# A weight ring of twenty 1 MB slots in place of ten 2 MB slots, in a two-layer diffusion backbone with a mixture of experts

## The chip, the cores and the metric

The kernel runs on one core of one Trainium2 chip. The metric is the device time of one execution in microseconds, lower is better. Everything is float32.

## What is computed

Two layers act on 256 latent tokens of 1024 values. Layer 0 mixes tokens by differential attention over latent and context tokens, layer 1 by centred pooling. After each mixer comes a mixture of 16 experts of which every token uses two. Cut to the part that the change touches:

```python
def moe_ffn(h, router_w, router_b, wg, wu, wd):       # h: 256 x 1024; wg, wu, wd: 16 x 1024 x 1024
    eidx, ew = route(h, router_w, router_b)           # two experts and two weights for each token
    ...                                               # the tokens of one expert are gathered into xb
    def expert_block(args):
        xb, e = args
        return (jax.nn.silu(xb @ wg[e]) * (xb @ wu[e])) @ wd[e]
    ...                                               # weighted sum back into the tokens

for i in range(DEPTH):                                # DEPTH = 2
    yl = diff_attention(...) if i % 4 == 0 else pool_mixer(hl, pool_w[j], pool_scale[j])
    xl = deepnorm_update(xl, yl, g1, ln_g[i, 0], ln_b[i, 0])
    y2 = moe_ffn(xl * (1.0 + sc2) + sh2, router_w, router_b, moe_wg[i], moe_wu[i], moe_wd[i])
    xl = deepnorm_update(xl, y2, g2, ln_g[i, 1], ln_b[i, 1])
```

The kernel computes every expert for its own tokens, in up to 64 slots for each expert. The weights of the experts are 2 layers x 16 experts x 3 matrices x 4 MiB = 402.65 MB, all of which must be read once from memory.

## The kernel before

The program is written by hand for each engine, with semaphores between them. The order of work on an engine is the order of the code.

**The ring.** `ring` is one SBUF buffer of RING = 10 slots, each of UNIT = 4096 values on each of 128 partitions, which is 2 MB (2.097 million bytes). A **unit** is one half of one expert matrix: 512 rows of 1024 values. An expert has EU = 6 units: two of moe_wg, two of moe_wu, two of moe_wd. Units are numbered through the program by v: 0 to 95 are layer 0's experts, 96 (POOL_UNIT) is the pooling layer's tables, 97 to 192 are layer 1's experts. `ring_slot` (L270) gives unit v the slot (v + 2) mod 10 and the number of times that this slot has been filled.

**Loading.** SP issues all weight DMAs, in order of v (`load_expert`, L391). In front of each stands `slot_free` (L376): the first ten units wait for parts of the attention that use the ring as scratch, and all others wait until unit v - 10 has been used (`used`, L279). One DMA brings a whole unit. Partition p gets the rows 4p to 4p + 3 of the half matrix, which lie next to one another in memory, so one partition's share is one run of 16 KB. Each DMA ends with an increment of `ring_loaded_{slot}`.

**Using.** On PE, `expert` (L785) runs for each expert: gate (bank 4) and up (bank 5) products from four units, then a gather of later tokens (L735), turning the hidden values (L759) and the slot weights (L765), the down product (bank 6) from two units, and the scatter (L751). A unit is used by `two_halves` (L739): four k-steps, each a pair of matmuls that write different halves of the partitions, so eight matmul instructions; the profile records each of them twice, so a unit is 16 of its MATMUL records (L743). `ring_unit` (L776) waits for the landing of the unit (`landed`), and the last matmul increments `unit_used`. ACT (L1050) takes the sigmoid once the gate product is complete (`used(act, v + 1)`), DVE (L1481) multiplies once the up product is complete (`used(dve, v + 3)`), copies the turned hidden values (L1496), and scales the down product (L1500, `used(dve, v + 5)`).

**Between the layers.** After expert 15 of layer 0 comes `pool_layer` (L845). Unit 96 holds pool_w (1 MB, as 1024 rows of 1 KB) in the first half of its slot, and the band table (128 rows of 4352 bytes) in the second; two DMAs with two semaphores, `pool_loaded` and `ring_loaded_{slot}`. POOL multiplies pool_w by a gate (L445) once it has landed. Before the pooling PE runs four matmuls whose result is not used (`keep_clock`, L682). `further_loads` and `further_experts` are loops for experts with more than 64 tokens; with these inputs they don't run.

The packing of rows to partitions in `load_expert`:

```python
src = (moe_wg, moe_wu, moe_wd)[n // 2][layer, e, (n % 2) * HALF:(n % 2 + 1) * HALF, :]
load(slot(s).rearrange("p (k n) -> p k n", k=4), src.rearrange("(p k) n -> p k n", p=P), sem(f"ring_loaded_{s}"))
```

Of the kernel before, what the change touches and what calls it, by code (L numbers as in the profile page):

```python
# [26 lines left out]
P = 128  # L27
D = 1024
KT = D // P
TOK = 256  # L30
TT = TOK // P
NB = 512
HALF = D // 2
# [16 lines left out]
UNIT = 4096  # L50
EU = 6
BAND = P + 8

# [11 lines left out]

POOL_UNIT = NE * EU
LAYER_BASE = [0, POOL_UNIT + 1]
PAIRS = NE // 2
# [77 lines left out]
def trunk(nc, x, c, ctx, c_ctx, mod_w, mod_b, ln_g, ln_b, attn_wqkv, attn_wo, attn_lam, attn_subln,  # L146
          pool_w, pool_scale, router_w, router_b, moe_wg, moe_wu, moe_wd, consts, rope, band, out):
    with ExitStack() as st:
# [121 lines left out]
        def ring_slot(v):  # L270

            return (v + SHIFT) % RING, v // RING + 1

# [46 lines left out]
        def first_unit(layer, e):  # L320

            return LAYER_BASE[layer] + e * EU

# [30 lines left out]
        def _(sp):  # L354
# [20 lines left out]

            def slot_free(v):  # L376

                if v < 2:
                    sp.wait_ge(sem("summed"), NSUM - 1 + v)
                elif v < 6:  # L380
                    sp.wait_ge(sem("oT_done"), 2 * TT)
                elif v == 6:
                    sp.wait_ge(sem("mix_done"), 2)
                elif v == 7:
                    normed(sp, 0, 1)
                elif v < RING:
                    sp.wait_ge(sem("unit_used"), NA - RING + v + 1)
                else:
                    used(sp, v - RING)

            def load_expert(layer, e):  # L391
                for n in range(EU):
                    v = first_unit(layer, e) + n
                    slot_free(v)
                    s, _ = ring_slot(v)
                    src = (moe_wg, moe_wu, moe_wd)[n // 2][layer, e, (n % 2) * HALF:(n % 2 + 1) * HALF, :]
                    load(slot(s).rearrange("p (k n) -> p k n", k=4), src.rearrange("(p k) n -> p k n", p=P),
                         sem(f"ring_loaded_{s}"))

# [11 lines left out]
            for layer in range(DEPTH):  # L411
                for e in range(NE):
                    load_expert(layer, e)
                further_loads(layer)
                if layer == 0:
                    slot_free(POOL_UNIT)
                    s, _ = ring_slot(POOL_UNIT)
                    load(slot(s)[:, 0:2048].rearrange("p (k n) -> p k n", k=KT),
                         pool_w[0].rearrange("g (k p) n -> p (g k) n", p=P), sem("pool_loaded"))
                    load(slot(s)[:, 2048:2048 + TT * 4 * BAND], band, sem(f"ring_loaded_{s}"))  # L420
            for t in range(TT):
# [8 lines left out]
        def _(pool):  # L430
# [9 lines left out]
            pool.wait_ge(sem("job_out"), 7)  # L440
            pool.wait_ge(sem("pool_loaded"), 16)
            pw = slot(ring_slot(POOL_UNIT)[0])[:, 0:2048].rearrange("p (g k n) -> p g k n", g=4, k=2)
            for g in range(4):
# [5 lines left out]
        def _(pe):  # L449
# [288 lines left out]

            def two_halves(b, lhs, w, k0):  # L739

                for k in range(4):
                    for h in range(2):
# [33 lines left out]
            def ring_unit(v):  # L776
                landed(pe, v)
                return slot(ring_slot(v)[0]).rearrange("p (k n) -> p k n", k=4)

# [5 lines left out]
            def expert(layer, e):  # L785
# [6 lines left out]
                for b in range(2):  # L792
                    for n in range(2):
                        if e2 == 0 and (b, n) == (0, 1):
                            pe.wait_ge(sem("xg_copied"), 4 * (gq + 2 * pr_ + 2))
                        two_halves(4 + b, x_in, ring_unit(v + 2 * b + n), 4 * n).then_inc(sem("unit_used"), 1)
                if pr_ + 1 < PAIRS:
# [12 lines left out]
                elif layer == DEPTH - 1:  # L810
                    pe.wait_ge(sem("lng_copied"), e2 + 1)
                for n in range(2):
                    two_halves(6, h_tile, ring_unit(v + 4 + n), 4 * n).then_inc(sem("unit_used"), 1)
                pe.wait_ge(sem("ys_ready"), q + 1)
# [30 lines left out]
            def pool_layer():  # L845

                v = POOL_UNIT
                pe.wait_ge(sem("pool_loaded"), 16)
                landed(pe, v)
                w = slot(ring_slot(v)[0])  # L850
                pw = w[:, 0:2048].rearrange("p (k n) -> p k n", k=KT)
                bd = w[:, 2048:2048 + TT * 4 * BAND].rearrange("p (t g n) -> p t g n", t=TT, g=4)
                keep_clock(5, 4)
# [16 lines left out]
                for t in range(TT):  # L870
                    for h in range(2):
# [10 lines left out]
                        if (t, h) == (1, 1):  # L882
                            last.then_inc(sem("unit_used"), 1)
                        pe.wait_ge(sem("xT8_act"), KT + 2 * h + 2)
# [22 lines left out]
        def _(act):  # L907
# [142 lines left out]
            def expert(layer, e):  # L1050
                v = first_unit(layer, e)
                used(act, v + 1)
                nc.scalar.activation(sig, bank(4), ACT.Sigmoid).then_inc(sem("sig_ready"), 1)  # L1053
# [53 lines left out]
        def _(dve):  # L1107
# [373 lines left out]
            def expert(layer, e):  # L1481
# [10 lines left out]
                dve.wait_ge(sem("silu_ready"), q + 1)  # L1492
                used(dve, v + 3)
                v_.tensor_tensor(hmid, hmid, bank(5), ALU.mult).then_inc(sem("h_ready"), 1)  # L1494
                dve.wait_ge(sem("hT_turned"), q + 1)
                v_.tensor_copy(work[:, NB:2 * NB], bank(7)).then_inc(sem("hTt_copied"), 1)  # L1496
                if e + 1 < NE:
                    weights_out(q + 1)
                used(dve, v + 5)
                v_.tensor_tensor(ysb, bank(6), gt[layer], ALU.mult).then_inc(sem("ys_ready"), 1)  # L1500
# [78 lines left out]
```

## Time and profile before

| | us |
|---|---|
| median of three runs | 1286.6 |
| lowest and highest run | 1284.5, 1288.28 |
| the profiled execution, its whole time | 1288.75 |
| the profiled execution, its span | 1286.4 |

PE is busy for 1178.4 us of the span, DVE for 379.5, ACT for 169.1 and POOL for 23.0. The granted clock of PE is full in most of the span.

The stages, by the timeline: conditioning and attention to 334 us; the first norm, the router and the first gathers to 355; experts of layer 0 from 355 to 792; norm, pooling, second norm and router to 837; experts of layer 1 from 837 to 1274; the last norm and the stores to 1286. To read the profile for this case, two clocks have to be laid side by side: at what pace PE uses the units, and at what pace the DMAs bring them. The first is read from the chain of waits, the second from the time of issue and the time to landing of single DMAs and from the windows, whose last number is the rate in GB/s.

### The profile page before, as it was taken

What the parts mean: (1) busy time and instruction counts of PE and PEld (TensorE: products, weight loads), DVE (VectorE), ACT (ScalarE), POOL (GpSimd) and SP (SyncE); (2) the same over time, 40 slices, a digit from 0 to 9 for tenths busy, and PEclk for the clock granted to TensorE, in tenths of its full rate; (3) what the DMA queues carried; (4) which work ended last, traced back from release to release, by engine and by line L of the source; (5) the groups of instructions that cost most, each with busy time, mean ns of one, the idle gap of its engine ahead of it and who ended that gap; (6) DMA issues with size and microseconds to landing.
All of it is one profiled execution on the core that took longest, in us unless ns stands there. A gap on an engine that the chain in (4) does not pass through costs nothing.

```text
span 1286.4 us, 12344 instructions
## 1 busy us (share of the span) xinstructions
PE 1178.4 (92%) x5277; PEld 508.7 (40%) x5277; DVE 379.5 (29%) x781; ACT 169.1 (13%) x398; POOL 23.0 (2%) x28
## 2 busy tenths in 40 slices
PE   5999999889899999999999998999999999999995
PEld 1444344445543343333343334733343333333331
DVE  1497898872411111111111103411111111111113
ACT  0201123341310010000010002410010000010000
POOL 0001100000000000000000001000000000000000
PEclk9799999968899999999999999899999999999998
DMA  9778868701999999999999999989999999999993
GB/s 326 290 260 297 325 234 294 287 2 51 430 383 429 427 428 428 427 428 427 427 428 427 429 427 418 419 366 428 426 429 427 430 425 429 426 428 429 425 428 165
DMA packets 54940, 476.27 MB, mean 370 GB/s; under 512 B 5034, under 2 KB 6458, under 8 KB 30308
## 3 DMA queue, kind: packets, MB, share of 16 engines
q1 hardware_dynamic: 42632, 433.04, 80.4%
q0 software_dynamic: 10560, 41.94, 8.9%
q8 instruction: 44, 0.72, 0.2%
q10 hardware_dynamic: 1692, 0.46, 0.2%
q14 instruction: 12, 0.10, 0.0%
HBM read 474.38 MB, written 1.05 MB: 370 GB/s over the span
## 4 chain that ended last, share of the span: by engine, by line
PE 76%; DMA 11%; DVE 9%; issue 2%; ACT 2%; SPq 0%; DVEq 0%
PE ps L743 47%; PE ps L535 5%; PE ps L735 5%; DMA ring<-in_mod_w 5%; PE ps L751 4%; DMA ring<-in_moe_wu 3%; DMA ring<-in_moe_wd 3%; DVE modp L1164 3%; PE ps L600 2%; PE ps L564 2%; DVE work L1496 2%; DVE work L1500 2%; PE ps L458 1%; PE ps L759 1%; PE ps L582 1%
## 5 line engine op out<-in xcount | busy, mean ns | idle before, releaser
L743 PE MATMUL ps<-ring,tra 128*64 128x512 f32 x2048 | 447.0, 594 | 3.0 <-DMA ring<-in_moe_wu 1.9
L743 PEld LDWEIGHTS ps<-ring,tra 128*64 128x64 f32 x2048 | 145.9, 137 | 299.1 <-issue 293.1
L743 PE MATMUL ps<-ring,work 128*64 128x512 f32 x1024 | 227.2, 595 | 29.4 <-DVE work L1496 29.2
L743 PEld LDWEIGHTS ps<-ring,work 128*64 128x64 f32 x1024 | 82.7, 137 | 153.2 <-issue 115.4
L535 PE MATMUL ps<-ring 128*128 128x512 f32 x320 | 141.6, 596 | 0.7 <-ACT ring L935 0.7
L1164 DVE SCALAR_TENSOR_TENSOR modp<-ring,modp 128x512 f32<-128x512 f32 x140 | 105.3, 752 | 5.0
L1491 DVE TENSOR_TENSOR work<-ps,work 128x512 f32<-128x512 f32 x32 | 22.1, 692 | 283.4 <-ACT work L1053 283.4
L535 PEld LDWEIGHTS ps<-ring 128*128 128x128 f32 x320 | 59.3, 190 | 77.4 <-issue 76.4
L1053 ACT ACTIVATE work<-ps 128x512 f32<-128x512 f32 x32 | 19.1, 597 | 532.7 <-PE ps L743 532.7
L751 PE MATMUL ps<-work,extra 64*128 64x512 f32 x256 | 63.6, 615 | 25.1 <-DVE work L1500 25.1
L1046 ACT ACTIVATE tra<-ps,cols 128x128 f32<-128x128 f32 x128 | 48.2, 456 | 246.4 <-PE ps L735 246.4
L1494 DVE TENSOR_TENSOR work<-work,ps 128x512 f32<-128x512 f32 x32 | 22.0, 688 | 182.0 <-PE ps L743 182.0
L735 PEld LDWEIGHTS ps<-extra,xn 128*128 128x128 f32 x512 | 65.0, 206 | 25.6 <-issue 22.7
L735 PE MATMUL ps<-extra,xn 128*128 128x128 f32 x512 | 70.7, 296 | 2.7 <-DVE extra L1405 2.7
L751 PEld LDWEIGHTS ps<-work,extra 64*128 64x128 f32 x256 | 22.0, 186 | 68.4 <-DVE work L1500 53.3
L1500 DVE TENSOR_TENSOR work<-ps,gt 128x512 f32<-128x512 f32 x16 | 11.1, 692 | 115.7 <-PE ps L743 115.7
L1500 DVE TENSOR_TENSOR work<-ps,rows 128x512 f32<-128x512 f32 x16 | 11.1, 692 | 115.4 <-PE ps L743 115.4
L1496 DVE COPY work<-ps 128x512 f32<-128x512 f32 x32 | 22.1, 692 | 51.0 <-PE ps L759 51.0
L989 ACT ACTIVATE work<-ps,small 128x512 f32<-128x512 f32 x32 | 21.7, 683 | 67.6 <-DVE small L1302 67.6
L508 PE MATMUL ps<-modp,cst 128*12 128x512 f32 x40 | 21.6, 623 | 5.5 <-DVE modp L1164 3.0
L1301 DVE TENSOR_REDUCE small<-ps 128x2 f32<-128x1024 f32 x16 | 19.5, 1221 | 11.9 <-PE ps L564 11.8
L564 PE MATMUL ps<-ring 64*128 64x512 f32 x64 | 22.7, 792 | 0.0
(177 smaller groups left out, 651.0 us busy)
## 6 DMA issues: line engine op xcount, KB each, us to landing
ring<-in_moe_wg SPq DMA_DIRECT2D x64, 2048.0 KB, 25.7
ring<-in_moe_wu SPq DMA_DIRECT2D x64, 2048.0 KB, 24.7
ring<-in_moe_wd SPq DMA_DIRECT2D x64, 2048.0 KB, 24.0
ring<-in_mod_w POOLq DMA_DIRECT2D x20, 2048.0 KB, 9.6
ring<-in_attn_wqkv SPq DMA_DIRECT2D x6, 2048.0 KB, 13.8
ring<-in_mod_w SPq DMA_DIRECT2D x4, 2048.0 KB, 18.6
ring<-in_attn_wo SPq DMA_DIRECT2D x2, 2048.0 KB, 9.1
xn<-in_x SPq DMA_DIRECT2D x1, 1024.0 KB, 17.2
```

What stands on the lines that cost most here:

```text
L535: last = mm(bank(g % 2), hT[:, k, t * P:t * P + P], w[:, k, :], start=(k == 0), stop=(k == KT - 1))
L564: last = mm(bank(score_bank(s) + n), qT[j][rows_n, h, t * P:t * P + P], kT[rows_n, HPJ * j + h, :], start=True, stop=True)
L600: last = mm(bank(2 * t + h), oT[t][:, k, :], wo[:, k, :], start=(k == 0), stop=(k == KT - 1))
L735: last = mm(bank(bk, 0, P, k * P, k * P + slots), xn[:, c0:c0 + P], sgat[:, t, 0:slots], start=(t == 0), stop=(t == TT - 1), skip_group_ch ...
L743: last = mm(ps[SLOTS * h:SLOTS * h + SLOTS, b, :], lhs(k0 + k), w[:, k, h * NB:(h + 1) * NB], start=(k0 + k == 0), stop=(k0 + k == KT - 1) ...
L751: last = mm(bank(2 * t + h), sw[SLOTS * h:SLOTS * h + SLOTS, t * P:t * P + P], ysb[SLOTS * h:SLOTS * h + SLOTS, :], start=False, stop=True ...
L1046: nc.scalar.activation(xg[i // 2 % 2][:, kk, :], bank(bk, k * P, k * P + P), ACT.Identity, bias=one(bcol[2 * layer], kk, 1), scale=one(aco ...
L1164: ins = v_.scalar_tensor_tensor(out=acc, in0=w[:, k, :], scalar=ck, in1=acc, op0=ALU.mult, op1=ALU.add)
L1491: v_.tensor_tensor(hmid, bank(4), sig, ALU.mult).then_inc(sem("silu_ready"), 1)
L1494: v_.tensor_tensor(hmid, hmid, bank(5), ALU.mult).then_inc(sem("h_ready"), 1)
L1496: v_.tensor_copy(work[:, NB:2 * NB], bank(7)).then_inc(sem("hTt_copied"), 1)
L1500: v_.tensor_tensor(ysb, bank(6), gt[layer], ALU.mult).then_inc(sem("ys_ready"), 1)
```

## The change

A slot is now handled as two halves of 1 MB. Units keep their places in the ring, but the numbers v now count halves ("parts"): an expert has PARTS = 12, the ring HALVES = 20, the pooling tables are parts 192 and 193, layer 1 begins at 194. Each part has its own DMA, its own `ring_loaded_{s}` semaphore, its own wait on PE and its own increment of `unit_used`. Part n of a unit brings the rows 4p + 2n and 4p + 2n + 1 to partition p, a run of 8 KB; the runs of one DMA now lie 16 KB apart in memory. The matmuls, their order and their operands stay as they are. The first twenty parts wait for what the first ten units waited for. The tables of the pooling layer get one part each, and band's DMA now waits for its own part's release; `pool_loaded` goes.

```diff
+HALVES = 2 * RING
+PARTS = 2 * EU
...
-            return (v + SHIFT) % RING, v // RING + 1
+            return (v + 2 * SHIFT) % HALVES, v // HALVES + 1
+
+        def half_slot(s):
+
+            return ring[:, s * UNIT // 2:(s + 1) * UNIT // 2]
...
-            def slot_free(v):
-
+            def slot_free(part):
+
+                v = part // 2
...
-                    used(sp, v - RING)
+                    used(sp, part - HALVES)
...
-                for n in range(EU):
+                for n in range(PARTS):
                     v = first_unit(layer, e) + n
                     slot_free(v)
                     s, _ = ring_slot(v)
-                    src = (moe_wg, moe_wu, moe_wd)[n // 2][layer, e, (n % 2) * HALF:(n % 2 + 1) * HALF, :]
-                    load(slot(s).rearrange("p (k n) -> p k n", k=4), src.rearrange("(p k) n -> p k n", p=P),
-                         sem(f"ring_loaded_{s}"))
+                    i, k0 = n // 2, n % 2 * 2
+                    src = (moe_wg, moe_wu, moe_wd)[i // 2][layer, e, (i % 2) * HALF:(i % 2 + 1) * HALF, :]
+                    load(half_slot(s).rearrange("p (k n) -> p k n", k=2),
+                         src.rearrange("(p k) n -> p k n", p=P)[:, k0:k0 + 2, :], sem(f"ring_loaded_{s}"))
...
-                    load(slot(s)[:, 0:2048].rearrange("p (k n) -> p k n", k=KT),
-                         pool_w[0].rearrange("g (k p) n -> p (g k) n", p=P), sem("pool_loaded"))
-                    load(slot(s)[:, 2048:2048 + TT * 4 * BAND], band, sem(f"ring_loaded_{s}"))
+                    load(half_slot(s).rearrange("p (k n) -> p k n", k=KT),
+                         pool_w[0].rearrange("g (k p) n -> p (g k) n", p=P), sem(f"ring_loaded_{s}"))
+                    slot_free(POOL_UNIT + 1)
+                    load(half_slot(s + 1)[:, 0:TT * 4 * BAND], band, sem(f"ring_loaded_{s + 1}"))
...
-            def two_halves(b, lhs, w, k0):
-
-                for k in range(4):
+            def two_halves(b, lhs, w, k0, count=4):
+
+                for k in range(count):
...
-                return slot(ring_slot(v)[0]).rearrange("p (k n) -> p k n", k=4)
+                return half_slot(ring_slot(v)[0]).rearrange("p (k n) -> p k n", k=2)
...
-                    for n in range(2):
-                        if e2 == 0 and (b, n) == (0, 1):
+                    for n in range(4):
+                        if e2 == 0 and (b, n) == (0, 2):
                             pe.wait_ge(sem("xg_copied"), 4 * (gq + 2 * pr_ + 2))
-                        two_halves(4 + b, x_in, ring_unit(v + 2 * b + n), 4 * n).then_inc(sem("unit_used"), 1)
+                        two_halves(4 + b, x_in, ring_unit(v + 4 * b + n), 2 * n, 2).then_inc(sem("unit_used"), 1)
...
-                for n in range(2):
-                    two_halves(6, h_tile, ring_unit(v + 4 + n), 4 * n).then_inc(sem("unit_used"), 1)
+                for n in range(4):
+                    two_halves(6, h_tile, ring_unit(v + 8 + n), 2 * n, 2).then_inc(sem("unit_used"), 1)
...
                         if (t, h) == (1, 1):
-                            last.then_inc(sem("unit_used"), 1)
+                            last.then_inc(sem("unit_used"), 2)
...
-                used(act, v + 1)
+                used(act, v + 3)
...
-                used(dve, v + 3)
+                used(dve, v + 7)
...
-                used(dve, v + 5)
+                used(dve, v + 11)
```

In SP's queue, at the start of layer 0's experts, this stood before (a row is a DMA, its shape, what it waits for, and how many alike follow):

```order
L356 DMA ring<-in_moe_wg 128x4096 [waits summed] x2
L356 DMA ring<-in_moe_wu 128x4096 [waits oT_done] x2
L356 DMA ring<-in_moe_wd 128x4096 [waits oT_done] x2
L356 DMA ring<-in_moe_wg 128x4096 [waits mix_done]
L356 DMA ring<-in_moe_wg 128x4096 [waits norm_dve,norm_act]
L356 DMA ring<-in_moe_wu 128x4096 [waits unit_used] x2
L356 DMA ring<-in_moe_wd 128x4096 [waits unit_used] x2
```

And this stands there now:

```order
L362 DMA ring<-in_moe_wg 128x2048 [waits summed] x4
L362 DMA ring<-in_moe_wu 128x2048 [waits oT_done] x4
L362 DMA ring<-in_moe_wd 128x2048 [waits oT_done] x4
L362 DMA ring<-in_moe_wg 128x2048 [waits mix_done] x2
L362 DMA ring<-in_moe_wg 128x2048 [waits norm_dve,norm_act] x2
L362 DMA ring<-in_moe_wu 128x2048 [waits unit_used] x4
L362 DMA ring<-in_moe_wd 128x2048 [waits unit_used] x4
```

The order of the matrices and the kinds of waits are the same; every DMA has become two of half the size. On PE, at the beginning of the first expert of layer 0, this stood before:

```order
L743 MATMUL ps<-ring,tra 64x512 [waits ring_loaded_2,swT_copied,xg_copied]
L743 MATMUL ps<-ring,tra 64x512 x7
L743 MATMUL ps<-ring,tra 64x512 [waits ring_loaded_3,xg_copied]
L743 MATMUL ps<-ring,tra 64x512 x7
L743 MATMUL ps<-ring,tra 64x512 [waits ring_loaded_4]
```

And this now:

```order
L752 MATMUL ps<-ring,tra 64x512 [waits ring_loaded_4,swT_copied,xg_copied]
L752 MATMUL ps<-ring,tra 64x512 x3
L752 MATMUL ps<-ring,tra 64x512 [waits ring_loaded_5]
L752 MATMUL ps<-ring,tra 64x512 x3
L752 MATMUL ps<-ring,tra 64x512 [waits ring_loaded_6,xg_copied]
L752 MATMUL ps<-ring,tra 64x512 x3
L752 MATMUL ps<-ring,tra 64x512 [waits ring_loaded_7]
```

The matmuls are the same ones in the same order; a wait for a landing stands after every fourth instead of after every eighth.

## Rows read from the trace of the kernel before

**Rows 1.** The page: span, PE's busy time, the rate in 40 slices of 32 us.

```profile
span 1286.4 us, 12344 instructions
...
PE 1178.4 (92%) x5277; PEld 508.7 (40%) x5277; DVE 379.5 (29%) x781; ACT 169.1 (13%) x398; POOL 23.0 (2%) x28
...
GB/s 326 290 260 297 325 234 294 287 2 51 430 383 429 427 428 428 427 428 427 427 428 427 429 427 418 419 366 428 426 429 427 430 425 429 426 428 429 425 428 165
```

**Rows 2.** Chain of waits, two experts of layer 0: start us, us, what.

```profile
464.67 13.88 PE ps L743 x64
...
492.03 13.88 PE ps L743 x64
```

**Rows 3.** Issue by SP of unit 10, and its time to landing in us.

```profile
L356 SPq DMA_DIRECT2D ring<-in_moe_wd x1: 328/328/328, 358.8 to 358.8; - x1
...
DMA to landing us min/median/max: 7.7/7.7/7.7
```

**Rows 4.** The same of unit 95, layer 0's last.

```profile
L356 SPq DMA_DIRECT2D ring<-in_moe_wd x1: 328/328/328, 745.4 to 745.4; - x1
...
DMA to landing us min/median/max: 40.2/40.2/40.2
```

**Rows 5.** The same of unit 107 and of unit 192, layer 1's last.

```profile
L356 SPq DMA_DIRECT2D ring<-in_moe_wd x1: 328/328/328, 840.3 to 840.3; - x1
...
DMA to landing us min/median/max: 7.9/7.9/7.9
...
L356 SPq DMA_DIRECT2D ring<-in_moe_wd x1: 328/328/328, 1226.8 to 1226.8; - x1
...
DMA to landing us min/median/max: 40.4/40.4/40.4
```

**Rows 6.** PE's timeline, last expert of each layer: start, us, what, idle before.

```profile
775.80 3.65 PE L743 MATMUL ps<-ring,tra 128*64 128x512 f32 x16 [0.86 <-DMA ring<-in_moe_wu]
...
785.68 3.65 PE L743 MATMUL ps<-ring,work 128*64 128x512 f32 x16 [0.18 <-DMA ring<-in_moe_wd]
...
1257.54 3.65 PE L743 MATMUL ps<-ring,tra 128*64 128x512 f32 x16 [1.03 <-DMA ring<-in_moe_wu]
...
1263.71 7.23 PE L743 MATMUL ps<-ring,work 128*64 128x512 f32 x32 [0.78 <-DVE work L1496]
```

**Rows 7.** Windows: stretch, length, busy by engine, granted clock, DMA share, GB/s.

```profile
20.00:25.00 5.00, 5.00 (x20) 0.98 (x12) 0.69 (x1) 0.00 (x0) 0.00 (x0) 1.00 1.05 387
354.00:362.00 8.00, 7.44 (x38) 3.13 (x38) 1.59 (x7) 1.51 (x4) 0.00 (x0) 1.00 0.66 238
400.00:500.00 100.00, 93.95 (x456) 37.17 (x458) 13.59 (x33) 6.91 (x16) 0.00 (x0) 1.00 1.01 428
835.00:845.00 10.00, 9.44 (x49) 4.29 (x50) 2.25 (x8) 2.11 (x5) 0.00 (x0) 1.00 0.55 205
```

**Rows 8.** Timeline: SP's first issue after attention; PE's first units of each layer.

```profile
316.08 0.81 SPq L356 DMA_DIRECT2D ring<-in_moe_wu  x2
...
355.12 13.95 PE L743 MATMUL ps<-ring,tra 128*64 128x512 f32 x64 [0.56 <-ACT tra L1046]
...
836.58 13.95 PE L743 MATMUL ps<-ring,tra 128*64 128x512 f32 x64 [0.56 <-ACT tra L1046]
```

**Rows 9.** Issues of pool_w and band (ns), and time to landing of the two.

```profile
L356 SPq DMA_DIRECT2D ring<-in_pool_w x1: 382/382/382, 748.8 to 748.8; - x1
L356 SPq DMA_DIRECT2D ring<-in_band x1: 32157/32157/32157, 749.3 to 749.3; - x1
...
DMA to landing us min/median/max: 39.7/40.2/40.6
```

**Rows 10.** Timeline of POOL and PE in the pooling layer.

```profile
788.70 4.93 POOL L445 TENSOR_TENSOR ring<-ring,modp 128x512 f32<-128x512 f32 x4 [557.71 <-DMA ring<-in_pool_w]
...
792.38 3.67 PE L685 MATMUL ps<-cst 128*128 128x512 f32 x8 [0.26 <-issue]
...
803.03 1.97 PE L879 MATMUL ps<-ring,tra 128*128 128x256 f32 x8
```

## What I expected, written before the changed kernel had run

> **What bounds the kernel now.** I read the page first, then the chain of waits, then the windows, then the issues of the DMA queue.
>
> The page says two things at once. PE is busy 92% of the span, and the DMAs move 427 or 428 GB/s in nearly every slice from 386 us on [rows 1]. The whole question lies in the two stretches in which the experts' weights stream: 355 to 792 us and 837 to 1274 us.
>
> The chain of waits runs through PE. One expert repeats there every 27.37 us (464.67 to 492.03), and no DMA is in it [rows 2]. An expert needs 6 units of 2 MB (2.097 MB in decimal). While the queue is never empty, the DMAs land one per 4.93 us. In layer 0 unit 10 was issued at 358.8 and landed 7.7 us later, and unit 95 was issued at 745.4 and landed 40.2 us later: (785.6 - 366.5)/85 = 4.93 us [rows 3, 4]. In layer 1 units 107 and 192 give, unrounded, (1267.2 - 848.2)/85 = 4.93 us again [rows 4, 5]. So six units take 29.6 us and PE takes 27.4 us. PE is the faster one, and gains 2.2 us on the stream with every expert. The ring's head start of ten units hides this until the last expert of the layer. There PE meets the stream: it waits 0.86 us for the last unit of moe_wu and 0.18 us for the last of moe_wd in layer 0, and 1.03 us in layer 1 [rows 6]. **Both bounds meet at the end of each layer within about 1 us.** A slower stream therefore shows almost in full, and a faster stream shows up to about 1 us a layer and no more. That a transfer issued at 745.4 lands after 40.2 us [rows 4] says that the queue holds 40 us of work by then.
>
> The stream itself has two holes. Each is at the start of a layer: the ring is full, everything issued has landed, and SP waits until PE has used its first unit. In 354 to 362 us the DMAs moved 238 x 8 = 1.90 MB where 428 GB/s would be 3.42 MB: 3.6 us idle. In 835 to 845 us they moved 2.05 of 4.28 MB: 5.2 us idle [rows 7]. SP issues again at 358.8 and 840.3, both 3.7 us after the expert's first matmul (355.12, 836.58) [rows 3, 5, 8].
>
> **The change, part by part.** *Release by halves, at the start.* Four units are 64 recorded matmuls and take 13.88 us [rows 2], so a unit of 16 takes 3.47 us and a half of 8 takes 1.73 us. The first release comes 1.73 us earlier and the stream restarts that much earlier, once per layer. Gain: 1.73 us of stream each. Room: in layer 0 the hole is 3.6 us, so it shrinks and does not close.
>
> *Waiting by halves, at the end.* After the last landing PE now has 8 matmuls rather than 16: 1.83 us instead of 3.65 us [rows 6]. Gain: 1.8 us a layer, as long as the last landing is what PE waits for.
>
> *Twice as many rows in the queue.* A transfer of 2 MB is 128 rows of 16 KB, 8 on each engine, and one completion packet. As two of 1 MB it is 256 rows of 8 KB, 16 on each engine, and two completion packets. Bytes are the same. The trace has no rows of 8 KB, so I bound the cost of a row from other sizes. At 20 to 25 us only rows of 2 KB are in flight, the fourth transfer of mod_w, and the rate is 387 GB/s against 428 in 400 to 500 us [rows 7]. Per 2 MB that is 5.42 against 4.90 us, 0.52 us for 64 - 8 = 56 more rows on each engine: **9.3 ns a row**. The other end is pool_w, rows of 1 KB. It was issued at 748.8 and landed 39.7 us later, at 788.5, 2.9 us after the last unit of the experts [rows 4, 9]. 1 MB in rows of 16 KB would take 2.47 us, so 60 more rows cost 0.43 us: 7.1 ns a row. This is one landing read to 0.1 us, while the first is a rate over 5 us, so I take 9.3 ns. The completion packet: band is 34 KB on each engine with one completion, and landed 40.6 us after 749.3, at 789.9, 1.3 us after pool_w [rows 9], and at 37.6 us a MB per engine those bytes take 1.31 us. Nothing is left beyond the 0.1 us to which the landings are read; I take 0.07 us as its upper bound. I count the extra completion as one more row. So a unit becomes 9 x 9.3 = 84 ns longer, 4.93 to 5.01 us. Bounds: 8 x 7.1 = 57 ns, with completions free; and 8 x 9.3 + 70 = 145 ns.
>
> The Trainium skill ("DMA: Bandwidth & Descriptors", section "iDMA fabric") gives 408.7 GB/s for a stream from SP of 1 MiB transfers with rows of 4 KiB; no run here shows such a stream. An estimate from it and the 428 here: 0.23 us a unit for 24 rows and one completion, 9/25 of which is 83 ns, and the sum below would be the same +7 us rather than the +3 us of the 57 ns.
>
> *The sum, layer 0.* The first eight units (issued from 316.08 on [rows 8]) end 0.7 us later, inside the hole: 3.6 - 1.7 - 0.7 = 1.2 us of it remain. So the restart is 1.73 us earlier. Then 86 units (10 to 95) take 86 x 0.084 = 7.2 us more. Last landing: 785.6 - 1.7 + 7.2, 5.5 us later. PE ends the expert with 1.8 us less behind it: 789.33 (785.68 + 3.65) becomes 793.0, **+3.7 us** [rows 6]. The path from the last part of moe_wu (775.80 + 5.3, then 1.8 of matmuls, 2.4 of the hidden chain, 7.3 of moe_wd) gives 792.7, just below.
>
> *Between the layers.* This is PE, DVE and ACT work on the new residual, 47.2 us from 789.33 to 836.58. It moves as a block. pool_w and band land 5.6 us later, band at 795.5; PE's keep_clock matmuls, which stood at 792.38, want it at 796.1. POOL's gating took 4.93 us from 788.70; it now ends near 799 and is wanted near 807 (803.03 + 3.7) [rows 10]. Nothing is added.
>
> *Layer 1.* First expert at 840.3. SP's first release is at 840.3 + 3.7 - 1.7, 1.9 us later than before (unrounded). The ring is full by then: the stream comes 5.5 + 10 x 0.084 = 6.3 us later, of the hole 5.2 + 1.9 - 6.3 = 0.8 us is left. Again 86 units, +7.2 us; last landing 1267.2 + 9.1 = 1276.3; 8 matmuls more end at 1278.2 instead of 1270.94 [rows 6]: **+7.3 us**. Written as a formula with x the extra time of a unit: 172 x - 7.1 us. The 7.1 us is the two earlier restarts and the two shorter ends.
>
> *At no cost.* PE gets 12 waits and releases an expert in place of 6: four units run in 13.95 us without a gap at the three waits inside [rows 8], and PE now waits for the stream anyway. SP issues one DMA in 0.33 us where one is wanted every 2.5 us. SP stood 32.16 us in the issue of band, with pool_w's 64 rows an engine and some seven units ahead of it [rows 9], so the queue takes a limited number of rows. With twice the rows SP will stand in an issue oftener, with only half the bytes queued. That is still four units or 20 us, and behind SP's waiting issue stand only later loads of the same stream.
>
> The profiled execution took 1288.75 us for a span of 1286.4; the median of the runs is 1286.6. I add to the median: 1286.6 + 7.3 = 1293.9.
>
> **The rivals.** *Rows cost nothing at this size.* Then x = 0, and the stream restarts earlier, ends earlier, and PE's own pace decides: only the waits of 0.86, 0.18 and 1.03 us go, 1286.6 - 2.1 = 1284.5 us. For it: both rates could be set by something else in the early phase. Against it: 387 and 428 GB/s differ with both shares over 1. Somewhere between, up to x = 64 ns, the result is within 3.9 us. The Trainium skill ("DMA: Bandwidth & Descriptors", section "Specifications") names 512 B as the smallest transfer for full rate, by which this rival would hold; the trace's 387 GB/s at 2 KB disagrees.
>
> *A half costs more than its rows.* A completion that holds up its engine, or reads that jump over 8 KB in memory. At the upper bound, 145 ns, the sum is 172 x 0.145 - 7.1 = +17.8 us, 1304 us; at 250 ns it would be 1322 us. Against it: band's landing.
>
> *The gain side wins.* Slots come free by halves and the ring is better filled. This decides only if x is under 41 ns, where 172 x = 7.1, and it is worth at most the 2.1 us above. So no case gives faster by over 0.3% unless a transfer itself becomes faster, which no row suggests.
>
> **How the numbers follow.** 0.3% is 3.9 us, about what a measurement of this kernel can tell from no change. Forecast, x from 64 to 145 ns: 0.69. Rows nearly free, x under 64 ns, between 1284.5 and 1290.5: 0.23. A half dearer than 145 ns: 0.05. A faster stream: 0.03. The range takes in the upper bound and part of the second case: 1286.5 to 1304. Faster 0.03, same 0.23, slower 0.74.
>
> **What would show it.** The rate in 400 to 500 us should fall from 428 to near 421 GB/s, and the packets of q1 rise by 24,576 rows. PE should wait for DMAs from about expert 13 on, some 2.7 us an expert. Layer 1's first expert should start 3 to 4 us later than 836.58, and the holes near 358 and 841 should shrink to about 1 us. The prediction is wrong if the rate stays at 427 or 428, if the last landings come earlier, or if the stream shows new holes.

## The result, and the profile after

The changed kernel is slower by 0.9%. Its median is 1294.99 us over six runs (1293.97 to 1298.05), against 1284.95 us (1276.97 to 1288.28) for the kernel before on the same chip. The ratio is 1.0088 with a 95% interval of 1.0058 to 1.0118. The forecast was 1293.9 us. The profiled execution took 1293.99 us.

From the page of the changed kernel, what answers [rows 1]: the span, the rate in 40 slices, the packets of the weight queue.

```profile
span 1291.5 us, 12537 instructions
...
GB/s 325 289 236 294 323 253 276 287 23 113 412 405 421 421 421 421 420 421 420 421 421 421 421 421 413 410 399 421 421 421 421 421 420 421 421 421 421 421 421 186
...
q1 hardware_dynamic: 70280, 433.05, 81.7%
```

Where 427 and 428 stood, 420 and 421 stand now. The weight queue has 27,648 packets more than before: 24,576 rows, and 192 more completions on each of 16 engines. The windows that answer [rows 7] (stretch, length, busy by engine, granted clock, DMA share, GB/s):

```profile
20.00:25.00 5.00, 4.54 (x22) 1.31 (x22) 1.16 (x2) 0.00 (x0) 0.00 (x0) 1.00 1.05 387
354.00:362.00 8.00, 8.00 (x40) 3.24 (x38) 0.69 (x1) 0.60 (x1) 0.00 (x0) 1.00 0.89 306
400.00:500.00 100.00, 94.02 (x458) 36.83 (x456) 13.99 (x33) 6.90 (x16) 0.00 (x0) 1.00 1.01 421
835.00:845.00 10.00, 9.44 (x54) 4.92 (x54) 1.59 (x7) 3.15 (x9) 0.00 (x0) 1.00 0.86 319
```

The stream is slower while it runs, with the DMAs just as busy (1.01), and its two holes are smaller. What answers [rows 3], [rows 4] and the band row of [rows 9], the issue and the time to landing of the first part of unit 10, of the last two parts of unit 95, and of band:

```profile
L362 SPq DMA_DIRECT2D ring<-in_moe_wd x1: 328/328/328, 353.5 to 353.5; - x1
DMA to landing us min/median/max: 7.2/7.2/7.2
...
L362 SPq DMA_DIRECT2D ring<-in_moe_wd x2: 2132/2135/2138, 758.5 to 760.7; - x2
DMA to landing us min/median/max: 27.6/27.8/28.0
...
L362 SPq DMA_DIRECT2D ring<-in_band x1: 17604/17604/17604, 766.5 to 766.5; - x1
DMA to landing us min/median/max: 26.4/26.4/26.4
```

The second part of unit 10 was issued at 355.2 and landed 8.0 us later, at 363.2. The last part of unit 95 landed at 760.7 + 28.0 = 788.7. So a part takes (788.7 - 363.2)/170 = 2.503 us and a unit 5.006 us, where [rows 3, 4] gave 4.93. At the end of the layer SP now stands 2.1 us in each issue, and transfers land 28 us after their issue rather than 40.

PE's timeline, end of layer 0 and end of layer 1, against [rows 6]:

```profile
770.54 1.94 PE L752 MATMUL ps<-ring,tra 128*64 128x512 f32 x8 [0.55 <-DMA ring<-in_moe_wu]
773.81 1.94 PE L752 MATMUL ps<-ring,tra 128*64 128x512 f32 x8 [1.33 <-DMA ring<-in_moe_wu]
776.14 1.94 PE L752 MATMUL ps<-ring,tra 128*64 128x512 f32 x8 [0.39 <-DMA ring<-in_moe_wu]
778.63 1.94 PE L752 MATMUL ps<-ring,tra 128*64 128x512 f32 x8 [0.55 <-DMA ring<-in_moe_wu]
781.42 0.75 PE L768 MATMUL ps<-cst,work 128*128 128x128 f32 x4 [0.86 <-DVE work L1503]
782.96 8.78 PE L752 MATMUL ps<-ring,work 128*64 128x512 f32 x32 [0.78 <-DVE work L1505]
792.53 1.99 PE L760 MATMUL ps<-work,extra 64*128 64x512 f32 x8 [0.79 <-DVE work L1509]
...
1264.14 1.94 PE L752 MATMUL ps<-ring,tra 128*64 128x512 f32 x8 [0.54 <-DMA ring<-in_moe_wu]
...
1268.60 7.38 PE L752 MATMUL ps<-ring,work 128*64 128x512 f32 x32 [0.78 <-DVE work L1505]
1276.78 1.99 PE L760 MATMUL ps<-work,extra 64*128 64x512 f32 x8 [0.80 <-DVE work L1509]
```

PE meets the stream and takes each part of moe_wu as it lands: a unit's half of matmuls, 1.94 us, then a wait of about 0.55 us. One row is new in kind. The 32 down matmuls of the last expert took 8.78 us in layer 0 and 7.38 us in layer 1. In layer 0 the second part of moe_wu also came late: PE waited 1.33 us for it.

**Stages.** The attention ahead of the experts is the same code in every kernel here, yet its end moved between 347 and 356 us from run to run, with the later stages moving along. So I compare stages from PE's timeline: layer 0 is the time from the first expert's first matmul to the start of expert 15's scatter, "between" goes from there to layer 1's first expert, layer 1 is counted like layer 0. Times are in us; the edits of the experiments are below.

| kernel | first expert | layer 0 | between | layer 1 | sum | to before |
|---|---|---|---|---|---|---|
| before | 355.12 | 435.01 | 46.45 | 435.15 | 916.61 | |
| after | 351.54 | 440.99 | 45.20 | 439.05 | 925.24 | +8.6 |
| after, second look (e0_parts) | 349.57 | 441.28 | 46.64 | 439.00 | 926.92 | +10.3 |
| e1_rows8_whole | 355.18 | 441.39 | 46.60 | 440.89 | 928.88 | +12.3 |
| e2_parts_coarse | 348.60 | 441.09 | 50.73 | 441.20 | 933.02 | +16.4 |
| e3_parts_contig | 346.95 | 439.98 | 45.26 | 438.88 | 924.12 | +7.5 |
| e4_rows4 | 353.67 | 452.15 | 46.35 | 452.10 | 950.60 | +34.0 |
| e5_half_bytes | 352.69 | 433.49 | 46.45 | 433.74 | 913.68 | -2.9 |
| e7_parts_clock | 348.93 | 438.97 | 43.75 | 441.26 | 923.98 | +7.4 |
| e6_hybrid | 356.05 | 434.94 | 46.41 | 433.75 | 915.10 | -1.5 |
| e9_hybrid_again | 351.64 | 433.56 | 46.53 | 433.74 | 913.83 | -2.8 |
| e8_hybrid_ends | 347.71 | 433.88 | 45.30 | 433.94 | 913.12 | -3.5 |

The column "between" has a spread of its own. The gathers just ahead of layer 1's first expert took 6.53 us in the kernel before, 5.28 in the changed kernel, 6.74 in e0_parts and 3.84 in e7_parts_clock, by how long PE's granted clock stood at 0.50 there. So the sum of one trace moves by up to 3 us with that clock. The two layers alone give +9.9 us for the changed kernel and +10.1 for e0_parts.

### The profile page after: what moved, and what is told of

Read it like the earlier page. It is cut to its first block, busy times and chain, and to the rows that moved or that the text cites. A ratio compares the mean times of both kernels' runs of the same rounds, so it can differ in the third digit from the quotient of the medians.

```text
span 1291.5 us, 12537 instructions
## 1 busy us (share of the span) xinstructions
PE 1174.3 (91%) x5277; PEld 503.4 (39%) x5277; DVE 378.9 (29%) x781; ACT 168.7 (13%) x398; POOL 23.0 (2%) x28
## 4 chain that ended last, share of the span: by engine, by line
PE 72%; DMA 13%; DVE 10%; issue 2%; ACT 2%; SPq 0%; DVEq 0%
PE ps L752 46%; PE ps L544 6%; PE ps L744 5%; DMA ring<-in_mod_w 5%; PE ps L760 4%; DMA ring<-in_moe_wu 4%; DMA ring<-in_moe_wd 4%; DVE modp L1173 3%; PE ps L609 2%; DVE work L1509 2%; DVE work L1505 2%; PE ps L768 1%; PE ps L573 1%; PE ps L467 1%; PE ps L591 1%
## 5 line engine op out<-in xcount | busy, mean ns | idle before, releaser
L768 PE MATMUL ps<-cst,work 128*128 128x128 f32 x128 | 20.9, 286 | 1.7 <-DVE work L1503 1.7
```

Of the source, the lines that this page charges most:

```text
L768: last = nc.tensor.transpose(bank(7, 0, P, k * P, k * P + P), every[:, k, :], ident)
```

## Experiments: is it the rows?

**The change again.** The changed kernel itself, run beside the first experiments.

> The changed kernel itself, beside the kernel before on the same chip, as the base for the others of this group. Rate of the stream 421 GB/s in 400 to 500 us, and 8 to 10 us longer than the kernel before.

Measured: 1293.66 us against 1284.6, ratio 1.0063 (1.0040 to 1.0087), rate 421. The slowdown repeats.

**Rows of 8 KB with transfers of 2 MB.** The kernel before with another packing:

```diff
-load(slot(s).rearrange("p (k n) -> p k n", k=4), src.rearrange("(p k) n -> p k n", p=P), ...)
+load(slot(s).rearrange("p (h m) -> p h m", h=2), src.rearrange("(h p k) n -> p h (k n)", h=2, p=P), ...)
```

> The kernel before with one edit: a DMA still brings a whole unit of 2 MB with one completion, but each partition's 16 KB come as two runs of 8 KB from two places of the same 2 MB. The matmuls so meet weight rows in another order and the output is not the reference's. Theory A, each row in the queue costs its engine a fixed time: 8 more rows a unit, at the 76 ns a unit that the changed kernel shows less one completion, gives a stream of about 421.5 GB/s, no gain from halves, so 172 x 0.07 = 12 us more than the kernel before. Theory B, the extra transfer with its completion is what costs: the rate stays at 428 GB/s and the time is that of the kernel before.

Measured: 1296.97 us, ratio 1.0085 (1.0055 to 1.0116). Its window and queue rows:

```profile
400.00:500.00 100.00, 93.92 (x456) 37.18 (x458) 13.54 (x34) 6.92 (x17) 0.00 (x0) 1.00 1.01 421
...
q1 hardware_dynamic: 67208, 433.04, 81.1%
```

The number of transfers, the waits and the releases are those of before; only the rows differ, and the rate is 421 again. Unit 11 landed at 371.5 and unit 95 at 792.0: (792.0 - 371.5)/84 = 5.006 us. For the kernel before the same two landed at 371.4 and 785.6, 4.931 us. Eight more rows on each engine cost 75 ns, **9.4 ns a row**. The changed kernel, which also has twice the transfers and completions, has the same 5.006 us, so the extra transfer and completion cost nothing that these rows can show. The time agrees with theory A of the expectation, and theory B is out.

**Each part one contiguous MB.** Does the 16 KB pitch between the 8 KB runs cost anything?

```diff
-src.rearrange("(p k) n -> p k n", p=P)[:, k0:k0 + 2, :]
+src[128 * k0:128 * k0 + 256, :].rearrange("(p k) n -> p k n", p=P)
```

> The changed kernel, but each 1 MB transfer reads one contiguous megabyte (rows 2p and 2p + 1 of a quarter matrix) in place of runs of 8 KB that lie 16 KB apart. The matmuls meet weight rows in another order and the output is not the reference's. If the jumps in memory cost nothing, the rate is 421 GB/s and the time that of the changed kernel, 8 to 10 us over the kernel before. If they are the cost, the rate returns to 427 GB/s or more and the time is 2 us under the kernel before.

Measured: 1295.6 us, ratio 1.0071 (1.0043 to 1.0098), rate 421. The jumps cost nothing that the rate or the time shows.

**Rows of 4 KB.** The same parts as 4 KB rows, to see whether the cost goes on by the row:

```diff
-src.rearrange("(p k) n -> p k n", p=P)[:, k0:k0 + 2, :]
+src[128 * k0:128 * k0 + 256, :].rearrange("(k p) n -> p k n", p=P)
```

> As the run with contiguous megabytes, but in rows of 4 KB: 16 more rows a unit on each engine than the changed kernel, the same number of transfers. Output not the reference's, since the weight rows come in another order. Theory A (a fixed time for each row, 9.3 ns): 149 ns more a unit, a rate near 409 GB/s, and 172 x 0.149 = 26 us more than the changed kernel, about 34 us over the kernel before. Theory B (only transfers cost): the changed kernel's time.

Measured: 1319.42 us, ratio 1.0256 (1.0217 to 1.0295). A window, the queue, and one of PE's waits (us in total, times, longest):

```profile
400.00:500.00 100.00, 94.03 (x459) 36.97 (x457) 13.99 (x33) 6.90 (x16) 0.00 (x0) 1.00 1.03 409
...
q1 hardware_dynamic: 119432, 433.05, 83.1%
...
PE ps L752 <- DMA ring<-in_moe_wu: 24.7, 38, 1.7
```

Per 2 MB, 428, 421 and 409 GB/s are 4.90, 4.98 and 5.13 us, and 387 GB/s at 2 KB [rows 7] is 5.42. With 8, 16, 32 and 64 rows on each engine the steps are 10, 9.1 and 9.1 ns a row, from rates read to 1 GB/s. Within that reading, which is 1 to 2 ns a row in the first step, one straight line holds from 16 KB down to 2 KB. The first three points come from 100 us windows, and the prediction's 5 us window lies on their line.

**Half the bytes.** Where does PE end if no weight is late?

```diff
-load(slot(s).rearrange("p (k n) -> p k n", k=4), src.rearrange("(p k) n -> p k n", p=P), ...)
+load(slot(s)[:, 0:UNIT // 2], src[0:HALF // 2, :].rearrange("(p k) n -> p (k n)", p=P), ...)
...
-w[:, k, h * NB:(h + 1) * NB]
+w[:, k % 2, h * NB:(h + 1) * NB]
```

> The kernel before with one megabyte a unit in place of two: the DMA loads half of the rows, and the matmuls use each of them twice, so half of the weights is left out and the output is not the reference's. It shows PE's own pace with no stream behind it. If the kernel before is bound by PE up to the waits at the end of each layer, this is 2.1 us faster than the kernel before, with experts 27.37 us apart; if the stream holds PE in a way that the waits don't show, it is faster by more.

Measured: 1281.79 us, ratio 0.9970 (0.9952 to 0.9989), and PE waits for no weight. This floor is 3 us under the kernel before. A better stream can give no more than that.

## Experiments: where the rest lies

**Parts on the DMA side only.** The changed kernel, but waiting and releasing by whole units:

```diff
-slot_free(v)
+slot_free(v | 1)
...
 landed(pe, v)
+landed(pe, v | 1)
```

> The changed kernel with its 1 MB transfers, but PE waits for both halves of a unit before it starts on it, and SP waits for both halves to be used before it issues either. The stream's rate should be the changed kernel's, 421 GB/s. If halves give what the prediction counted (1.73 us earlier restart and 1.8 us shorter end in each layer), this is 7 us slower than the changed kernel; if the earlier restart gains nothing, 3.6 us; if neither gives anything, equal.

Measured: 1300.12 us, ratio 1.0117 (1.0088 to 1.0147), 6.5 us more than e0_parts. Layer 1 took 441.20 us against 439.00, so **the finer ends and restarts are worth 2.2 us there**. Layer 0 took 441.09 against 441.28: nothing there. The rest of the difference is in the stretch between the layers, 50.73 us in the profiled run, where PE stood 5.23 us before its keep_clock matmuls. The granted clock fell to 0.50 behind that stall, and the matmuls took 5.71 us in place of 3.67. A late table is not the cause: pool_w had landed at 788.1 and band at 789.4, and the stall lasted to 796.9. Its cause stays open. Only the profiled run shows it, though all four runs of this kernel (1296.39 us and up) lie above all five of e0_parts (1295.08 and down). So the 6.5 us must not be read as the 7 us of the expectation.

**The clock at the end of layer 0.** What made 32 matmuls take 8.78 us? Windows of the changed kernel:

```profile
780.00:782.00 2.00, 1.14 (x8) 0.56 (x4) 0.69 (x1) 0.00 (x0) 0.00 (x0) 1.00 1.00 418
782.00:784.00 2.00, 1.22 (x6) 0.34 (x6) 0.69 (x1) 0.00 (x0) 0.00 (x0) 0.88 0.99 404
784.00:786.00 2.00, 2.00 (x8) 0.59 (x6) 0.00 (x0) 0.00 (x0) 0.00 (x0) 0.50 1.05 388
786.00:788.00 2.00, 2.00 (x10) 0.67 (x8) 0.00 (x0) 0.00 (x0) 0.00 (x0) 0.76 1.06 379
788.00:790.00 2.00, 2.00 (x12) 0.72 (x10) 0.00 (x0) 0.00 (x0) 0.00 (x0) 1.00 1.07 399
```

The granted clock is the third number from the end of a row. It went from 1.00 to 0.50 of full speed, which is 1.2 GHz in place of 2.4, and back. In the windows before, PE had the short waits for parts shown above and then idled 0.86 and 0.78 us around the turning of the hidden values. The kernel before kept 1.00 there, as did e1_rows8_whole and e2_parts_coarse, which wait by whole units; e0_parts and e3_parts_contig, which wait by parts, fell to 0.50 and 0.52. But e6_hybrid waits by parts too and kept 1.00, and so did e4_rows4, whose waits for moe_wu in the same expert are all longer than those of the changed kernel. These are the waits, and two windows of its down product:

```profile
784.07 1.94 PE L752 MATMUL ps<-ring,tra 128*64 128x512 f32 x8 [0.62 <-DMA ring<-in_moe_wu]
787.69 1.94 PE L752 MATMUL ps<-ring,tra 128*64 128x512 f32 x8 [1.69 <-DMA ring<-in_moe_wu]
790.26 1.94 PE L752 MATMUL ps<-ring,tra 128*64 128x512 f32 x8 [0.63 <-DMA ring<-in_moe_wu]
792.82 1.94 PE L752 MATMUL ps<-ring,tra 128*64 128x512 f32 x8 [0.62 <-DMA ring<-in_moe_wu]
...
798.00:800.00 2.00, 2.00 (x12) 0.72 (x10) 0.00 (x0) 0.00 (x0) 0.00 (x0) 1.00 1.05 394
800.00:802.00 2.00, 2.00 (x12) 0.57 (x8) 0.00 (x0) 0.00 (x0) 0.00 (x0) 1.00 1.05 373
```

So the short waits alone don't do it. As a trial, two records of filler matmuls per expert were put where expert 14 and expert 15 of layer 0 have nothing between the products and the turn:

```diff
 elif layer == DEPTH - 1:
     last_row(6, 6 + e2).then_inc(sem("lng_spread"), 1)
+else:
+    keep_clock(6, 1)
```

> The changed kernel with one more matmul, whose result is not used, on PE in experts 14 and 15 of layer 0, between the up product and the turning of the hidden values. Theory: in the changed kernel's layer 0 the granted clock fell to 0.5 for about 4 us in the last expert, after its waits for moe_wu and the idle time before the turn, and that cost 1.7 us in its down product (8.78 us where layer 1 takes 7.38). With the gap filled, as layer 1 has it filled, the down product takes 7.1 to 7.4 us, layer 0 is 1 to 1.7 us shorter from its first expert to its last, and the time 1 to 2 us under the changed kernel. Rival: the fall has another cause, and the product stays at 8.8 us.

Measured: 1291.63 us, ratio 1.0058 (1.0032 to 1.0085). Windows and timeline of this kernel:

```profile
782.00:784.00 2.00, 2.00 (x12) 0.71 (x10) 0.00 (x0) 0.00 (x0) 0.00 (x0) 1.00 1.04 381
784.00:786.00 2.00, 1.65 (x8) 0.34 (x6) 0.00 (x0) 0.00 (x0) 0.00 (x0) 1.00 1.07 383
...
776.99 1.12 PE L694 MATMUL ps<-cst 128*128 128x512 f32 x2
777.95 0.72 PE L768 MATMUL ps<-cst,work 128*128 128x128 f32 x4
779.45 5.37 PE L752 MATMUL ps<-ring,work 128*64 128x512 f32 x24 [0.78 <-DVE work L1507]
785.17 1.94 PE L752 MATMUL ps<-ring,work 128*64 128x512 f32 x8 [0.35 <-DMA ring<-in_moe_wd]
```

The clock stays at 1.00, the down product takes 785.17 + 1.94 - 779.45 = 7.66 us rather than 8.78, of which 0.35 is a wait for the last part, and layer 0 takes 438.97 us rather than 440.99 or 441.28. **The lower clock cost 1.1 us**, less than the 1.7 us of the expectation. The rest of those 2.0 and 2.3 us is something else: here the last part of moe_wu landed 426.19 us after the first expert's first matmul, and 427.09 and 427.37 us in the changed kernel and e0_parts. There PE waited 1.33 and 1.85 us for the second part of moe_wu in expert 15, and 0.56 us here. Why that part came late, no run here tells.

That the filler kept the clock up is not shown. This run differs from the changed kernel also in the late part, and e4_rows4, with longer waits and no filler, kept 1.00. A second profile with the filler, and one without it in which no part is late, would be needed.

Nor does the gain reach the end: layer 1 took 441.26 us where it had taken 439.0. Its first expert began at 831.65, and the ring's first fill went on landing until 839.7. The unit that takes the first freed slot was complete at 844.7, 13.1 us after the expert's first matmul where the changed kernel had 10.9. The sum of stages gained 1.3 and 2.9 us on the two profiles of the changed kernel, about what the stretch between the layers gave (43.75 us against 45.20 and 46.64). The medians gained 2.0 us on e0_parts in another set of runs, and the intervals of the two ratios overlap. So no gain of the whole time by the filler is shown.

**The best of both.** Rows of 16 KB in 2 MB transfers nearly everywhere, and parts of 1 MB only where a release or a wait ends something. Of the changed kernel:

```diff
+SPLIT = set(range(10, 14)) | set(range(90, 97)) | set(range(107, 111)) | set(range(187, 193))
...
+                    if v // 2 not in SPLIT:
+                        if n % 2 == 0:
+                            slot_free(v + 1)
+                            load(ring[:, s * UNIT // 2:(s + 2) * UNIT // 2].rearrange("p (k n) -> p k n", k=4),
+                                 src.rearrange("(p k) n -> p k n", p=P), sem(f"ring_loaded_{s}"))
+                        continue
```

> Rows of 16 KB and 2 MB transfers for most units, and halves only for the four units after each layer's restart and for the last six units of each layer (20 of 192 units, and the pooling tables). The stream keeps 427 to 428 GB/s. By the prediction's terms PE's own pace then decides and the waits of 0.86, 0.18 and 1.03 us go: 2 us faster than the kernel before. If halves gain nothing, equal to the kernel before.

Measured: 1280.13 us, ratio 0.9970 (0.9950 to 0.9991). Its end of layer 0:

```profile
778.24 1.94 PE L767 MATMUL ps<-ring,tra 128*64 128x512 f32 x8 [0.56 <-DMA ring<-in_moe_wu]
...
782.57 5.37 PE L767 MATMUL ps<-ring,work 128*64 128x512 f32 x24 [0.78 <-DVE work L1520]
788.26 1.94 PE L767 MATMUL ps<-ring,work 128*64 128x512 f32 x8 [0.32 <-DMA ring<-in_moe_wd]
```

Against e0_parts this is the same waiting at the ends with the row length given back. By the two ratios, 0.9970 and 1.0063, that is 12 us, near the 12.9 us of 172 units at 75 ns.

> The hybrid again, on the same chip as the run with halves at the ends alone. From the first run (ratio 0.997 to the kernel before) and from the stages, which put it 1.5 us under the kernel before between the first expert and the last, 2 to 4 us faster than the kernel before.

Measured: 1282.72 us against 1285.44, ratio 0.9972 (0.9953 to 0.9992). It repeats.

> As the hybrid, but with halves only in the last six units of each layer; the four units after each restart come whole, as in the kernel before. Against the hybrid it shows what an earlier restart is worth. If the restart gains the 1.7 us that was predicted, this loses it in the landings: unit 107 lands 11.6 us after layer 1's first matmul as in the kernel before, against 10.6 in the hybrid, and PE waits at the end of a layer. If the traces of the changed kernel are right, the restart gains 0 to 0.7 us, and this kernel is within 1 us of the hybrid and about 2 us faster than the kernel before.

With `SPLIT = set(range(90, 97)) | set(range(187, 193))`: 1280.54 us, ratio 0.9969 (0.9951 to 0.9986). The parts at the restarts add nothing. Splitting the last units of each layer is enough, and it reaches the floor of e5_half_bytes. This version beats both kernels, by 0.3% and, from the two ratios to the kernel before, 0.9969 and 1.0088, by 1.2%.

## Why the prediction was right, and which terms were off

**Both bounds meet at the end of the layer**: right. The floor is 3 us below the kernel before, and a slower stream showed almost in full. The first waits of layer 0 stand in expert 14, one later than I had said. Expert 15 waits 0.55 + 1.33 + 0.39 + 0.55 = 2.82 us, near the 2.7 forecast; expert 14 waits less than half of that:

```profile
745.68 1.94 PE L752 MATMUL ps<-ring,tra 128*64 128x512 f32 x8 [0.49 <-DMA ring<-in_moe_wu]
748.16 1.94 PE L752 MATMUL ps<-ring,tra 128*64 128x512 f32 x8 [0.54 <-DMA ring<-in_moe_wu]
...
758.10 1.94 PE L752 MATMUL ps<-ring,work 128*64 128x512 f32 x8 [0.24 <-DMA ring<-in_moe_wd]
```

**The term of 84 ns a unit**: 75 ns measured. The row itself was right, 9.4 against 9.3 ns. The ninth row, which I had put in for the extra completion, was not there. The two 86-unit terms are 12.9 us, not 14.4. The rival "rows cost nothing" falls with e1_rows8_whole; the rival "a half costs more than its rows" falls with e3_parts_contig and with the equal 5.006 us. The Trainium skill ("DMA: Bandwidth & Descriptors", section "Specifications") names 512 B as the smallest transfer for full rate; the 428, 421 and 409 GB/s at rows of 16, 8 and 4 KB disagree. The Trainium skill's rate for a stream of 1 MiB transfers with rows of 4 KiB (same page, section "iDMA fabric"), 408.7 GB/s, agrees with the 409 of e4_rows4.

**The shorter end, 1.8 us a layer**: layer 1 took 439.0 us with waits by halves and 440.9 or 441.2 without. Right in layer 1, where this difference holds the restart too. In layer 0 it took 440.99 us with them and 441.09 without (e2_parts_coarse): the lower clock took back 1.1 us, and the last weights landed 0.5 us later from the first matmul on.

**The earlier restart, 1.73 us a layer**: this is the term that failed. SP did issue earlier, at 353.51, which is 1.97 us after the first matmul rather than 3.7. But unit 10 was complete 11.7 us after that matmul, where before it took 11.4, and in layer 1 10.9 where it took 11.6. The step had carried over [rows 3]: a 2 MB transfer landed 7.7 us after its issue, so one of 1 MB should land 2.5 us sooner, after 5.3. It took 7.2 in layer 0 and, by the next rows, 6.4 in layer 1:

```profile
L362 SPq DMA_DIRECT2D ring<-in_moe_wd x1: 328/328/328, 839.7 to 839.7; - x1
DMA to landing us min/median/max: 6.4/6.4/6.4
```

The gain was used up: nothing came of it in layer 0, some 0.7 us in layer 1. The prediction also says that everything issued has landed when SP restarts. That was a misreading. The ring's first fill had landed by 359.6 in layer 0, and unit 10 was issued at 358.8. I had taken the loss as the time for which nothing was queued. The landings give a better measure: the time from the last landing of the fill to the completion of the next unit, less the pace of a unit (4.93 us before, 5.01 after), in us:

| kernel, layer | restart ahead of the fill's last landing | time lost |
|---|---|---|
| before, layer 1 | -0.1 | 3.1 |
| before, layer 0 | 0.8 | 2.0 |
| e0_parts, layer 1 | 1.3 | 2.6 |
| after, layer 0 | 2.6 | 2.1 |
| e0_parts, layer 0 | 2.7 | 2.3 |
| after, layer 1 | 3.2 | 0.7 |
| e7_parts_clock, layer 1 | 6.1 | 0.0 |

Going from 0.8 to 2.7 us ahead, the earlier restart gains nothing; that is where layer 0 stood before and after. In layer 0 the rate after the restart fell to 164 GB/s a second time, in 358 to 359 us. Why, no run here tells.

**The holes** were to shrink to 1.2 and 0.8 us. Over 26 us around each start, the missing bytes are 2.0 and 2.6 us of a stream of 421 GB/s, against 3.5 and 5.4 us of one of 428 before. They shrank, but not to what I had said.

**Between the layers, a block**: 45.20 and 46.64 us against 46.45. Layer 1's first expert came at 837.73, 1.15 us later than 836.58 and not 3 to 4; but attention had ended 3.6 us sooner in that run. Counted from layer 0's first expert it is 4.7 us later (486.19 us against 481.46), and 6.5 us in e0_parts, both above the 3.7 forecast.

**Not in the sum at all: the clock.** I had not asked whether the clock would hold in the last expert. Where it fell it cost 1.1 us of layer 0; what made it fall stays open.

The new sum: 12.9 for the rows, less 3.6 for the two ends, less 0.7 for the restart in layer 1, plus 1.1 for the clock, is +9.7 us. The two layers gave +9.9 and +10.1, the medians +10.0. **The terms were off in opposite directions**: the unit dearer by 9 ns than it was (1.5 us too much), and the restart and the clock (2.8 and 1.1 us too little). So the mechanism and the price of a row were right, and the forecast rise of 7.3 us was 2.7 us short. That the forecast came within 1.1 us of the median is luck in part: it started from 1286.6 us, where the median of the comparison was 1284.95.

## What to carry to other kernels

In a stream that runs near the DMA limit, the length of the row sets the rate, not the size of the transfer: keep the rows as long as the layout allows and split a transfer only where its own landing ends a wait. Before splitting for latency, find the two or three places where a wait ends last; here six units a layer bring all of the gain, and the other ninety only pay. And look at the granted clock behind the waits before a difference of 1 us is put down to them.

## What was not expected of the hardware

- A row costs each DMA engine a fixed 9 to 10 ns over its bytes from 16 KB down to 2 KB, and in a queue that stays full a transfer of 1 MB costs no more than half of one of 2 MB with the same rows (5.006 us per 2 MB either way).
- The queue of SP seems to take a limited number of rows; no run varied that alone. With rows of 16 KB, transfers landed 40 us after an issue of 0.33 us, and band's issue stood for 32.16 us [rows 9]. With 8 KB rows SP stood about 2.1 us in every issue at the end of the layer, band's took 17.6 us, and transfers landed after 28 us. No cost of it shows in the rates, and only later loads of the stream stand behind.
- A stream that had nearly run dry lost 2.0 to 2.6 us at its restart when the next transfer was issued 0.8 to 2.7 us ahead of the last landing, 0.7 us at 3.2 us ahead, and none at 6.1.
- A lone 1 MB transfer into an empty queue landed 4.8 us after its issue (e5_half_bytes, at 356.4 us). The first part of the changed kernel, with others about it, took 7.2.
- TensorE's granted clock fell to half within an expert in which PE was idle for no more than 1.33 us at a time (after; 1.85 us in e0_parts). In e4_rows4 it stayed full with idle times of up to 1.69 us in the same expert.
